# Recurrence and attention in blocks of their own, with gate slabs between their steps

## The chip, the cores and the metric

The kernel runs on one core of a Trainium2 chip (trn2). It is one program in Bass: every engine (PE or TensorE for matmuls, DVE or VectorE, ACT or ScalarE, POOL or GpSimd, SP or SyncE for issuing DMAs) has an instruction list of its own that it works off in order, and the lists are tied together by semaphores. The metric is device time of one execution in microseconds (us); lower is better. The kernel before ran three times: 2592.06, 2585.43 and 2591.16 us, median 2591.16.

## What is computed

One step of a streaming encoder layer for two request groups, a prompt of 1024 tokens and a sample of 64 new tokens after 128 cached ones (1088 tokens together, eight tiles of 128 and one of 64). D_MODEL is 1024. Cut to what matters here:

```python
h = rms_norm(x, pre_mix_gain)
a_q, a_k, a_v, i_q, i_k, i_w, b_q, b_f, b_i, b_g, c_q, gates = split(h @ w_in)   # gates: 3 * 1024 columns
# A: each query keeps its top-k keys by an indexer's score, 6 heads of 128, 2 kv heads
s = where(valid, q @ k_sel * HEAD_DIM ** -0.5, -inf);  y_a = softmax(s) @ v_sel
# B: gated linear recurrence, 6 heads, key and value width 128
f = lower_bound + (1 - lower_bound) * sigmoid(b_f);  b = cumsum(log(f))
o = (q * exp(b)) @ state + (decayed causal scores) @ v
state = exp(b_end) * state + (k * exp(b_end - b)).T @ v
y_b = rms_norm(o, hgrn_norm_gain) * silu(b_g)
# C: cross attention of 4 heads into 256 memory tokens -> y_c
g_a, g_b, g_c = split(sigmoid(gates))
merged = g_a * (y_a @ w_out_a) + g_b * (y_b @ w_out_b) + g_c * (y_c @ w_out_c)
x = x + rms_norm(merged @ w_out, ...);  then a squared-ReLU MLP of width 4096
```

## The kernel before

**Projections.** The program is a row of blocks, and between two blocks all engines meet. `block_project` works through a plan of weight slabs of 256 columns. A slab is loaded (1 MB, SP L172), rounded to its high part `w_hi` by ACT (L179), its low part `w_lo` is made by POOL (L186), and PE makes three products per pair of operands (hi by hi, hi by lo, lo by hi; L199) to keep fp32 accuracy. There are two slab buffers, so a slab's PE work covers the preparation of the next one. A slab of the form "features" has 6 bank units (2 times 128 features, by column groups of 384, 384 and 320 tokens), 24 matmuls each, so 144 matmuls a slab. ACT moves each finished bank to `b_stage` with the slab's function (L513), and SP stores it.

Block b1 makes the indexer's inputs, block b2 (`plan_second`) all the rest: 16 slabs of k, v, q, b_i, c_q, b_g and b_q, then 9 gate slabs with Sigmoid, then 3 slabs of kind "decay", then 3 gate slabs. Beside b2 the indexer runs: PE makes scores, and DVE finds each row's top-k (`index` steps, L753 to L764) and leaves an additive mask in SBUF (`bias`, for all tiles). A decay slab needs DVE for each bank (L564: f from the sigmoid, L567: 1 - f) and for scans of the logarithms (L574), and ACT takes the Ln of its six banks at its end (L519). DVE takes them in its list only behind the last top-k step. The staging buffers `ix_work` and `ix_qT` of the indexer carry the decay results to SP.

**Branches.** `block_branches` then goes over 54 slots, one for each head of each tile (`A_HEADS` = 6). In a slot stand: scores of one attention head (L1013), the mask and maximum on DVE (L1331), Exp on ACT (L1222), the turn of the probabilities on PE (L982), the products with the values once in three heads (L1036), parts of the memory attention, and two steps (one before, one behind the attention's share) of the recurrence. A tile's recurrence has 6 scaling steps (kinds 1, 2, 4, ... 64 with a `k` and a `q` step beside them; `stages(i)`): DVE makes differences `dif` (L1374, L1381, L1384, L1385), ACT takes Exp (L1203 to L1206), POOL multiplies them into `wk` (L1267 to L1276), PE makes 6 small fp32 products (L1090, two records each), and DVE copies the allowed parts into `smat` (L1405). At a tile's end come the output and state products (L1080, L1083, L1097), the mean square (ACT L1233, DVE L1453), its power on POOL (L1293, L1295), the scaling of 6 heads on ACT (L1249), the product with `bg` on POOL (L1300), the turn on PE (L1105) and the store.

**Merge.** `block_merge`'s stage splits y into high and low parts by pieces (ACT L1551, DVE L1589), multiplies by `w_out_a`, `w_out_b`, `w_out_c`, and DVE multiplies each bank by its stored gate (L1598). After it come the output projection and the MLP.

Of the kernel before, what the change touches and what calls it, by code (L numbers as in the profile page):

```python
# [7 lines left out]
P = 128  # L8
D_MODEL, SEQ, DEC, PAST, N_MEM = 1024, 1024, 64, 128, 256
HD, IDX_D = 128, 64  # L10
# [84 lines left out]
def build(nc, io):  # L95
    with ExitStack() as ctx:
# [18 lines left out]

        g.ident = g.sb("ident", [P, P])
        g.gains = g.sb("gains", [P, 3, KT])
        ring_semaphores(g)
        with ExitStack() as mid:
            g.bias = mid.enter_context(nc.sbuf_tensor("bias", [P, BIAS_OFF[N_TILE]], F32))  # L120
            with ExitStack() as first:
                weight_ring(g, first, "w1")
                g.h_hi = first.enter_context(nc.sbuf_tensor("h_hi", [P, KT, T_PAD], F32R))
                g.h_lo = first.enter_context(nc.sbuf_tensor("h_lo", [P, KT, T_PAD], F32R))
                with ExitStack() as c0:
                    g.m_hi = c0.enter_context(nc.sbuf_tensor("m_hi", [P, KT, N_MEM], F32R))
                    g.m_lo = c0.enter_context(nc.sbuf_tensor("m_lo", [P, KT, N_MEM], F32R))
                    plans = plan_first(g), plan_second(g)
                    block_norm(g, plans[0][:2])
                    block_project(g, "b1", plans[0], False, plans[1][:2])  # L130
                block_project(g, "b2", plans[1], True, [])
            block_branches(g)
# [25 lines left out]
def ring_semaphores(g):  # L158
    g.slab = 0
    g.arrived = [g.sem(f"arrived{i}") for i in range(N_TILE + N_MEM // P)]  # L160
    g.w_loaded = [g.sem("w_loaded0"), g.sem("w_loaded1")]
    g.w_rounded = g.sem("w_rounded")
    g.w_split = g.sem("w_split")

# [46 lines left out]
def block_norm(g, ahead):  # L211
    nc, io = g.nc, g.io
    NT = N_TILE + N_MEM // P
    with ExitStack() as ctx:
# [16 lines left out]
        with nc.Block() as block:  # L231
# [49 lines left out]
            def _(dve):  # L281
                nc.vector.memset(ss[:], 1.0).then_inc(zeroed, 1)
                for t in (g.h_hi, g.h_lo):
                    nc.vector.memset(t[:, :, T_ALL:T_PAD].bitcast(F32), 0.0)
# [79 lines left out]
def plan_second(g):  # L364
# [29 lines left out]
    n_late = 3  # L394
    gates = [(g.d_gate[j * 256:], OFF_G + j * 256) for j in range(3 * D_MODEL // 256)]
    for d, off in gates[:-n_late]:
        to_features(d, off, 1, ACT.Sigmoid)
# [4 lines left out]
    for d, off in gates[-n_late:]:  # L402
        to_features(d, off, 1, ACT.Sigmoid)
    return plan


def block_project(g, tag, plan, with_index, ahead):
# [13 lines left out]
    n_out = []  # L421
# [4 lines left out]
    with ExitStack() as ctx:  # L426
# [5 lines left out]
        stored = [g.sem(f"{tag}_stored{j}") for j in range(NS)]  # L432
# [4 lines left out]
        with nc.Block() as block:  # L437
            @block.sync
            def _(sp):
# [26 lines left out]
                for j in range(NS):  # L466
                    sp.wait_ge(stored[j], 16 * per[j])
# [30 lines left out]
            def _(act):  # L498
# [3 lines left out]
                for s, sl in enumerate(plan):  # L502
                    for n in range(first[s], first[s + 1]):
# [6 lines left out]
                        if n >= NS:  # L510
                            act.wait_ge(stored[n % NS], 16 * n_out[n - NS])
# [12 lines left out]
            def _(pe):  # L524
                for s, sl in enumerate(plan):
# [3 lines left out]
                    for n in range(first[s], first[s + 1]):  # L529
# [3 lines left out]
                        if sl.kind == "t":  # L533
                            c = slice(u[0] * P, (u[0] + 1) * P)
                            last = three_products(pe, g.ps[:, n % NB, 0:sl.cols],
# [87 lines left out]
def index_setup(g, ctx):  # L623
# [9 lines left out]
    ix.cnt = sb("ix_cnt", [P, 1])  # L633
    ix.in_, ix.turned, ix.kept, ix.scored = g.sem("ix_in"), g.sem("ix_turned"), g.sem("ix_kept"), g.sem("ix_scored")
# [9 lines left out]
    ix.n_in = 0  # L644
    return ix

# [60 lines left out]
def index_select(g, ix, dve):  # L707
# [32 lines left out]
    for i in range(N_TILE):  # L740
# [23 lines left out]
        link(v.tensor_scalar(sc, left, -1.0, MASKED, ALU.add, ALU.mult))  # L764

# [3 lines left out]
N_HEAD = N_TILE * A_HEADS  # L769
N_SLOT = N_HEAD + 4  # L770
# [9 lines left out]
STEP0 = [sum(len(stages(j)) for j in range(i)) for i in range(N_TILE + 1)]  # L780


def v_tiles(i):

    if i < TILE_P:
        return [(j, P) for j in range(i + 1)]
    return [(TILE_P, P), (TILE_P + 1, DEC)]


def block_branches(g):  # L790
    nc, io = g.nc, g.io
    V, S, G = nc.vector, nc.scalar, nc.gpsimd
    with ExitStack() as ctx:
        sb = lambda name, shape, dt=F32: ctx.enter_context(nc.sbuf_tensor("br_" + name, shape, dt))
# [1280 lines left out]
```

## Time and profile before

The three timed runs gave 2592.06, 2585.43 and 2591.16 us; the profiled execution has a span of 2590.3 us, 0.9 below their median.

| stretch, us | what runs | length, us |
|---|---|---|
| 42 to 183 | block b1 | 141 |
| 183 to 974.3 | block b2, 31 slabs | 791.3 |
| 977.1 to 1445.1 | block_branches | 468.0 |
| 1445.1 to 1691 | merge with the gates | 245.9 |
| 1691 to 2590 | output projection and MLP | 899 |

The profile's list of busy time and its 40 slices of the span (each digit is a busy share in tenths; PEclk the granted clock of TensorE in tenths of full speed):

```profile
PE 2391.7 (92%) x14604; PEld 2208.2 (85%) x14604; DVE 1303.8 (50%) x2275; ACT 724.3 (28%) x1334; POOL 707.6 (27%) x708
...
PE   6999999999999995778888699997999999999998
...
DVE  4113469999960513878777344416332332332335
...
PEclk8999999999999996889999899998999999999999
```

Slices 16 to 22 are the branch block. It is the one long stretch in which PE's digit is below 9.

### The profile page before, as it was taken

What the parts mean: (1) busy time and instruction counts of PE and PEld (TensorE: products, weight loads), DVE (VectorE), ACT (ScalarE), POOL (GpSimd) and SP (SyncE); (2) the same over time, 40 slices, a digit from 0 to 9 for tenths busy, and PEclk for the clock granted to TensorE, in tenths of its full rate; (3) what the DMA queues carried; (4) which work ended last, traced back from release to release, by engine and by line L of the source; (5) the groups of instructions that cost most, each with busy time, mean ns of one, the idle gap of its engine ahead of it and who ended that gap; (6) DMA issues with size and microseconds to landing.
All of it is one profiled execution on the core that took longest, in us unless ns stands there. A gap on an engine that the chain in (4) does not pass through costs nothing. (4 is left out here: it accounts for less than half of the span.)

```text
span 2590.3 us, 36896 instructions
## 1 busy us (share of the span) xinstructions
PE 2391.7 (92%) x14604; PEld 2208.2 (85%) x14604; DVE 1303.8 (50%) x2275; ACT 724.3 (28%) x1334; POOL 707.6 (27%) x708
## 2 busy tenths in 40 slices
PE   6999999999999995778888699997999999999998
PEld 5988799999999994566666599897998998998996
DVE  4113469999960513878777344416332332332335
ACT  5223422222122323444544211224221221221222
POOL 2432332121122113555444222115122122122112
PEclk8999999999999996889999899998999999999999
DMA  4352123222222325322210553314111111111103
GB/s 150 104 146 64 34 78 94 79 93 94 84 95 92 102 98 183 87 61 86 82 45 26 169 182 117 98 68 139 41 49 33 48 49 40 41 49 49 32 33 146
DMA packets 205526, 217.48 MB, mean 84 GB/s; under 512 B 25808, under 2 KB 185616, under 8 KB 205392
## 3 DMA queue, kind: packets, MB, share of 16 engines
q1 hardware_dynamic: 205392, 215.66, 26.4%
q8 instruction: 88, 1.44, 0.2%
q14 instruction: 46, 0.38, 0.0%
HBM read 155.26 MB, written 60.36 MB: 83 GB/s over the span
## 5 line engine op out<-in xcount | busy, mean ns | idle before, releaser
L186 POOL TENSOR_TENSOR w_lo<-w_raw,w_hi 128x2048 fp32r<-128x2048 f32 (+2 forms) x48 | 205.7, 4286 | 824.4 <-ACT w_hi L179 824.4
L199 PE MATMUL ps<-h_hi,w_lo 128*128 128x384 f32 (+1 forms) x960 | 313.1, 326 | 0.0
L199 PE MATMUL ps<-h_lo,w_hi 128*128 128x384 f32 (+1 forms) x960 | 312.9, 326 | 0.0
L199 PE MATMUL ps<-h_hi,w_hi 128*128 128x384 f32 (+1 forms) x960 | 312.8, 326 | 0.0
L1900 POOL TENSOR_TENSOR w_lo<-w_raw,w_hi 128x2048 fp32r<-128x2048 f32 x31 | 142.9, 4609 | 589.3 <-ACT w_hi L1924 589.3
L199 PE MATMUL ps<-w_hi,h_hi 128*128 128x256 f32 x1008 | 288.0, 286 | 7.8 <-PEq L437 4.1
L513 ACT ACTIVATE b_stage<-ps 128x256 f32<-128x256 f32 (+4 forms) x254 | 106.6, 420 | 665.6 <-PE ps L199 665.6
L199 PE MATMUL ps<-w_lo,h_hi 128*128 128x256 f32 x1008 | 287.0, 285 | 0.0
L199 PE MATMUL ps<-w_hi,h_lo 128*128 128x256 f32 x1008 | 286.9, 285 | 0.0
L199 PE MATMUL ps<-f_hi,w_hi 128*128 128x384 f32 (+1 forms) x768 | 251.2, 327 | 2.5 <-POOL ff_u_lo L1896 2.5
L199 PE MATMUL ps<-f_hi,w_lo 128*128 128x384 f32 (+1 forms) x768 | 251.1, 327 | 0.0
L199 PE MATMUL ps<-f_lo,w_hi 128*128 128x384 f32 (+1 forms) x768 | 250.9, 327 | 0.0
L1977 DVE TENSOR_TENSOR big<-big,ps 128x512 f32<-128x512 f32 x144 | 98.9, 687 | 272.0 <-PE ps L199 272.0
L199 PE MATMUL ps<-w_hi,ff_u_lo 128*128 128x512 f32 x576 | 224.2, 389 | 0.0
L199 PE MATMUL ps<-w_lo,ff_u_hi 128*128 128x512 f32 x576 | 224.2, 389 | 0.0
L199 PE MATMUL ps<-w_hi,ff_u_hi 128*128 128x512 f32 x576 | 224.1, 389 | 0.0
L199 PEld LDWEIGHTS ps<-w_hi,h_hi 128*128 128x128 f32 x1008 | 195.5, 194 | 10.9 <-issue 6.7
L1967 DVE TENSOR_TENSOR ff_relu_sq<-ff_relu_sq 128x384 f32<-128x384 f32 (+1 forms) x96 | 83.8, 873 | 238.1 <-ACT ff_relu_sq L1933 237.9
L199 PEld LDWEIGHTS ps<-w_lo,h_hi 128*128 128x128 f32 x1008 | 195.5, 194 | 0.0
L199 PEld LDWEIGHTS ps<-w_hi,h_lo 128*128 128x128 f32 x1008 | 195.3, 194 | 0.0
L199 PEld LDWEIGHTS ps<-h_hi,w_hi 128*128 128x128 f32 x960 | 180.2, 188 | 0.0
L199 PEld LDWEIGHTS ps<-h_hi,w_lo 128*128 128x128 f32 x960 | 180.2, 188 | 0.0
(219 smaller groups left out, 5078.0 us busy)
## 6 DMA issues: line engine op xcount, KB each, us to landing
w_raw<-in_w_in SPq DMA_DIRECT2D x34, 1024.0 KB, 5.6
w_raw<-in_w_up SPq DMA_DIRECT2D x16, 1024.0 KB, 5.5
w_raw<-in_w_down SPq DMA_DIRECT2D x16, 1024.0 KB, 5.1
d_gate<-b_stage SPq DMA_DIRECT2D x48, 192.0 KB, 1.8
gm_gate<-d_gate SPq DMA_DIRECT2D x48, 192.0 KB, 2.6
gm_y_raw<-d_y SPq DMA_DIRECT2D x8, 576.0 KB, 4.5
n_x<-in_x_prompt SPq DMA_DIRECT2D x8, 512.0 KB, 5.8
w_raw<-in_w_mem_kv SPq DMA_DIRECT2D x4, 1024.0 KB, 6.2
```

The lines of the kernel that those rows point to most:

```text
L186: engine.tensor_tensor(g.w_lo[:, s, 0:size], g.w_raw[:, s, 0:size], g.w_hi[:, s, 0:size].bitcast(F32), ALU.subtract).then_inc(g.w_split, 1)
L199: last = pe.matmul(out, left(a, kk), right(b, kk), start=(kk == 0 and n == 0), stop=(kk == k - 1 and n == 2))
L513: nc.scalar.activation(stage[0:r, n % NS, 0:c], g.ps[0:r, n % NB, 0:c], sl.func).then_inc(staged, 1)
L1900: G.tensor_tensor(g.w_lo[:, slot, :], g.w_raw[:, slot, :], g.w_hi[:, slot, :].bitcast(F32), ALU.subtract).then_inc(g.w_split, 1)
L1967: V.tensor_tensor(sq[:, u % 2, 0:n], relu[:, u % 2, 0:n], relu[:, u % 2, 0:n], ALU.mult).then_inc(sq_made, 1)
L1977: V.tensor_tensor(dst, dst, g.ps[:, 4 + d % B_DN, :], ALU.add).then_inc(acc_done, 1)
```

## The change

`block_branches` is taken apart. Three of the twelve gate slabs stay in b2 (2 before the three decay slabs, 1 behind), so that b2 has 22 slabs instead of 31. Four gate slabs are made inside a new `block_recurrence`, five inside a new `block_attention`, by a class `Filler`: it puts a given number of the slabs' matmuls into PE's list between the steps of the block, ACT moves the finished banks out, POOL makes `w_lo` of the next slab (in `block_recurrence` in four pieces of 512 columns), and SP loads and stores. The recurrence block has one step per tick, 80 steps in 86 ticks, with 48 matmuls of the filler first and 6 in each tick. The attention block has the 54 slots, with 96 matmuls first and 12 in each slot; the value products (now one per head) and the memory attention's outputs have PSUM banks of their own.

Further parts: gates are stored without Sigmoid (`ACT.Copy`), and the merge opens them on ACT (`open_gate`); the gain of the recurrence's norm moves from a POOL product (L1289) to a scale in the merge's split, behind a small load `head_gain`; the mask `bias` is stored to DRAM (`store_bias`, 9 DMAs, 2.4 MB) and read back per tile in two buffers; `h_hi` and `h_lo` are cut to 1088 tokens; the level steps' `dif` is one operation of 768, and their Exp two of 384.

```diff
+            gates = plan_gates(g)
+            beside_recurrence, beside_attention = gates[3:7], gates[7:]
+            plans = plan_first(g), plan_second(g, gates[:3])
...
+            block_project(g, "b2", plans[1], True, beside_recurrence[:2])
+            block_recurrence(g, Filler(g, "r", beside_recurrence, beside_attention[:2], [0, 1, 2, 3], 3))
+            block_attention(g, Filler(g, "a", beside_attention, [], [5, 6], 2))
...
-    for d, off in gates[:-n_late]:
-        to_features(d, off, 1, ACT.Sigmoid)
+    for sl in gates[:-1]:
+        plan.append(sl)
...
+                            if n == decays[0]:
+                                store_bias(g, ix, sp)
...
+    def fill(self, pe, count):
+        g, nb = self.g, len(self.banks)
+        for _ in range(count):
+            u, m = divmod(self.mm, self.n_mm)
+            if u == len(self.units):
+                return
+            s, (ft, c0, n, _) = self.units[u]
+            if m == 0:
+                if u % self.per_slab == 0:
+                    pe.wait_ge(g.w_split, self.n0 + s + 1)
+                if u >= nb:
+                    pe.wait_ge(self.evicted, u - nb + 1)
...
+LEAD_IN, PER_TICK = 48, 6
+N_TICK = Q_STEP[-1] + 8
...
+                fl.fill(pe, LEAD_IN)
+                for tick in range(N_TICK):
+                    late = tick in Q_STEP
+                    if late:
+                        fl.fill(pe, PER_TICK)
+                    if tick < len(STEPS):
+                        recur_step(tick)
+                    for i in at(lambda i: STEP0[i + 1], tick):
+                        recur_state(i)
+                    for i in at(lambda i: Q_STEP[i] + 6, tick):
+                        recur_out(i)
+                    if not late:
+                        fl.fill(pe, PER_TICK)
...
+                for n in range(N_SLOT):
+                    i, slot = divmod(n, A_HEADS)
+                    if n < N_HEAD:
+                        scores(n)
+                    fl.fill(pe, PER_SLOT // 2)
...
+                open_gate(0)
+                open_gate(1)
                 for u, (s, b, f, c0, n) in enumerate(units):
+                    if u + 2 < len(units):
+                        open_gate(u + 2)
```

On SP's list in block b2, around the first stores of a decay slab (`d_kk` and `d_cum` are the decay results in DRAM, `d_gate` the gates), the program before has:

```order
L465 DMA d_gate<-b_stage 128x384 x2
L465 DMA d_gate<-b_stage 128x320
L172 DMA w_raw<-in_w_in 128x8x256
L454 DMA d_kk<-ix_work 128x384
L454 DMA d_cum<-ix_qT 128x384
L454 DMA d_kk<-ix_work 128x384
```

After the change the same place, seven slabs earlier in the plan, has the stores of the mask behind the first pair:

```order
L475 DMA d_gate<-b_stage 128x320
L177 DMA w_raw<-in_w_in 128x8x256
L462 DMA d_kk<-ix_work 128x384
L462 DMA d_cum<-ix_qT 128x384
L669 DMA d_bias<-bias 128x128
L669 DMA d_bias<-bias 128x256
...
L669 DMA d_bias<-bias 64x192
```

The mask's stores, the first of which waits for the last top-k step, now stand ahead of the further decay stores and the next slab's load.

On PE's list inside the branch work (`br_wk` is the recurrence's scaled operand, `br_prob` the attention's probabilities), the program before has this, attention and recurrence by turns:

```order
L1013 MATMUL ps<-br_kT,br_qT 128x512
L1048 MATMUL ps<-br_mkT,br_cq 128x256 x2
L1036 MATMUL ps<-br_pT,br_val 128x384 x3
L1090 MATMUL ps<-br_wk 128x128 x6
L982 MATMUL ps<-ident,br_prob 128x128 x4
L1090 MATMUL ps<-br_wk 128x128 x6
```

In the new recurrence block (`hr_wk` is the same operand, L833 the filler's matmul on a gate slab):

```order
L1044 MATMUL ps<-hr_wk 128x128 x6
L833 MATMUL ps<-h_hi,w_hi 128x384
L833 MATMUL ps<-h_lo,w_hi 128x384
L833 MATMUL ps<-h_hi,w_lo 128x384
L833 MATMUL ps<-h_hi,w_hi 128x384
L833 MATMUL ps<-h_lo,w_hi 128x384
L833 MATMUL ps<-h_hi,w_lo 128x384
L1044 MATMUL ps<-hr_wk 128x128 x6
```

What stood between two recurrence steps was attention; now it is six gate matmuls, and the attention follows in a block of its own.

On ACT's list at the start of the merge (`gm_y_hi` is the high part of y, in pieces), the program before has:

```order
L1551 ACTIVATE gm_y_hi<-gm_y_raw 128x2x320 [waits gm_y_in0]
L1551 ACTIVATE gm_y_hi<-gm_y_raw 128x2x320 [waits gm_y_in1]
L1551 ACTIVATE gm_y_hi<-gm_y_raw 128x3x384 [waits gm_y_in0,gm_full]
L179 ACTIVATE w_hi<-w_raw 128x1024 [waits w_loaded0,gm_full]
```

After the change:

```order
L1789 ACTIVATE gm_y_hi<-gm_y_raw 128x2x320 [waits gm_y_in0]
L1789 ACTIVATE gm_y_hi<-gm_y_raw 128x2x320 [waits gm_y_in1]
L1801 ACT_TABLE_LOAD
L1801 ACTIVATE gm_gate<-gm_gate 128x384 [waits gm_gate_in0]
L1801 ACTIVATE gm_gate<-gm_gate 128x384 [waits gm_gate_in1]
```

The sigmoids of the gates, with a table load ahead of the first, stand behind all six pieces of the first split.

## Rows read from the trace of the kernel before

**Rows 1.** Windows of stages: window, length, busy (instructions) of PE, PEld, DVE, ACT, POOL, PEclk, DMA share, GB/s.

```profile
618.60:832.00 213.40, 213.40 (x1297) 213.40 (x1296) 135.93 (x182) 43.10 (x64) 41.63 (x9) 1.00 0.29 92
...
977.10:1002.60 25.50, 11.26 (x44) 7.48 (x44) 2.37 (x7) 9.90 (x20) 0.78 (x2) 0.59 1.01 325
1002.60:1445.10 442.50, 345.10 (x2034) 274.34 (x2034) 340.07 (x758) 197.93 (x457) 227.22 (x178) 0.90 0.23 65
1445.10:1472.00 26.90, 10.77 (x49) 10.13 (x49) 9.19 (x10) 6.95 (x8) 4.72 (x2) 0.67 0.65 202
```

**Rows 2.** Timeline of POOL in block b2, two gate slabs running: start, duration, operation.

```profile
620.92 4.63 POOL L186 TENSOR_TENSOR w_lo<-w_raw,w_hi 128x2048 fp32r<-128x2048 f32 x1 [19.09 <-ACT w_hi L179]
644.65 4.63 POOL L186 TENSOR_TENSOR w_lo<-w_raw,w_hi 128x2048 fp32r<-128x2048 f32 x1 [19.09 <-ACT w_hi L179]
```

**Rows 3.** Timeline of DVE from the last top-k step to the first decay steps.

```profile
758.70 0.25 DVE L764 TENSOR_SCALAR bias<-ix_work 64x192 f32<-64x192 f32 x1
836.87 2.37 DVE L564 TENSOR_SCALAR b_stage<-b_stage,fg_oml,fg_lb 128x384 f32<-128x384 f32 x1 [77.92 <-ACT b_stage L513]
...
840.96 0.48 DVE L564 TENSOR_SCALAR b_stage<-b_stage,fg_oml,fg_lb 128x384 f32<-128x384 f32 x1 [1.32 <-ACT b_stage L513]
```

**Rows 4.** Timeline of ACT at the end of the first decay slab.

```profile
856.26 1.28 ACT L519 ACT_TABLE_LOAD   x1
857.55 2.49 ACT L519 ACTIVATE b_stage<-b_stage 128x384 f32<-128x384 f32 x6
859.95 1.90 ACT L179 ACTIVATE w_hi<-w_raw 128x2048 fp32r<-128x2048 f32 x1
861.87 1.28 ACT L513 ACT_TABLE_LOAD   x1
```

**Rows 5.** Groups of POOL in the branch block: busy, mean ns of one, idle before and its releasers.

```profile
L1276 POOL TENSOR_TENSOR br_wk<-br_bq,br_ex 128x384 f32<-128x384 f32 x48 | 53.7, 1119 | 0.0
L1275 POOL TENSOR_TENSOR br_wk<-br_kk,br_ex 128x384 f32<-128x384 f32 x48 | 51.6, 1076 | 93.4 <-issue 52.1 <-PE ps L1090 31.7 <-ACT br_ex L1206 8.6
L1300 POOL TENSOR_TENSOR br_osb<-br_osb,br_bg 128x768 f32<-128x768 f32 x8 | 16.9, 2107 | 0.0
L1267 POOL TENSOR_TENSOR br_kp<-br_kk,br_exn 128x768 f32<-128x768 f32 x8 | 16.4, 2049 | 74.6 <-ACT br_ex L1204 74.6
L1270 POOL TENSOR_TENSOR br_wk<-br_bq,br_ex 128x768 f32<-128x768 f32 x8 | 14.8, 1855 | 19.2 <-PE ps L1090 19.2
...
L1295 POOL TENSOR_TENSOR br_ms<-br_ms,br_expo 128x6 f32<-128x6 f32 x8 | 11.9, 1488 | 0.7
L1293 POOL TENSOR_SCALAR br_ms<-br_ms 128x6 f32<-128x6 f32 x8 | 4.8, 598 | 0.7
```

**Rows 6.** Groups of DVE in the same stretch.

```profile
L1405 DVE COPY_PREDICATED br_smat<-br_masks,ps 128x384 f32<-128x384 int32 x112 | 62.0, 584 | 35.3 <-PE ps L1090 30.4 <-PE ps L1088 4.1
```

**Rows 7.** Groups of ACT in the same stretch.

```profile
L1206 ACT ACTIVATE br_ex<-br_dif 128x768 f32<-128x768 f32 x56 | 46.2, 840 | 24.8 <-DVE br_dif L1385 19.2 <-POOL br_wk L1268 3.3 <-DVE br_dif L1374 0.8
...
L1249 ACT ACTIVATE br_osb<-br_osb,br_ms 128x128 f32<-128x128 f32 x48 | 14.9, 389 | 41.8 <-POOL br_ms L1295 41.8
```

**Rows 8.** Timeline of PE inside the branch block (an fp32 product is two records).

```profile
1307.83 4.03 PE L1036 MATMUL ps<-br_pT,br_val 128*128 128x384 f32 x12
1311.70 1.50 PE L1090 MATMUL ps<-br_wk 128*128 128x128 f32 x12
...
1315.97 2.63 PE L1090 MATMUL ps<-br_wk 128*128 128x128 f32 x12 [2.00 <-DVE br_smat L1405]
```

**Rows 9.** Windows at the merge's first matmuls, columns as in rows 1.

```profile
1460.00:1463.00 3.00, 3.00 (x11) 3.00 (x10) 0.67 (x1) 0.92 (x2) 0.00 (x0) 0.50 1.06 369
1463.00:1466.00 3.00, 2.32 (x13) 2.00 (x12) 1.40 (x2) 1.83 (x2) 1.94 (x1) 0.99 0.45 139
```

**Rows 10.** Timeline of DVE at the start of the merge.

```profile
1467.17 1.01 DVE L1598 TENSOR_TENSOR big<-ps,gm_gate 128x384 f32<-128x384 f32 x2
```

**Rows 11.** Timeline of ACT there, the last piece of the first split.

```profile
1470.28 0.74 ACT L1551 ACTIVATE gm_y_hi<-gm_y_raw 128x640 fp32r<-128x640 f32 x1 [3.25 <-DMA gm_y_raw<-d_y]
```

More of the change, by code:

```diff
@@ L401, in plan_second, with plan_gates @@
                              [(ft, c0, n, 2 * j + ft) for ft in range(2) for c0, n in GROUPS], ACT.Sigmoid))
[L402 to L404 removed]
+    plan.append(gates[-1])
+    return plan
+def plan_gates(g):
+    w = g.io["w_in"][0]
+    return [SlabPlan("f", w_cols(w, OFF_G + j * 256, 256), 256, feature_units(g.d_gate, j * 256), ACT.Copy)
+            for j in range(3 * D_MODEL // 256)]
 def block_project(g, tag, plan, with_index, ahead):
@@ L431, in block_project @@
         rope_part, rope_done = g.sem(f"{tag}_rope_part"), g.sem(f"{tag}_roped")
-        stored = [g.sem(f"{tag}_stored{j}") for j in range(NS)]
+        stored, before = g.stored, list(g.stored_before)
+        g.stored_before = [b + 16 * k for b, k in zip(before, per)]
         ix = index_setup(g, ctx) if with_index else None
@@ L644, in index_setup, with store_bias @@
     ix.n_in = 0
-    return ix
+    per_tile = [2 if i < 2 else (1 if i < TILE_P else 0) + 2 * ((TOPK_P if i < TILE_P else TOPK_S) // 8) - 1 + 7
+                for i in range(N_TILE)]
+    ix.n_steps = sum(per_tile)
+    return ix
+def store_bias(g, ix, sp):
+    sp.wait_ge(ix.step, ix.n_steps)
+    for i in range(N_TILE):
+        sp.dma_start(g.d_bias[row_slice(i), 0:n_keys(i)],
+                     g.bias[0:rows(i), BIAS_OFF[i]:BIAS_OFF[i + 1]]).then_inc(ix.bias_out, 16)
 def index_loads(g, ix, sp):
@@ L883, in dcount, with at, done_before @@
+        def at(ticks, tick):
+            return [i for i in range(N_TILE) if ticks(i) == tick]
+        def done_before(tick):
+            return min(len(fl.units), (LEAD_IN + PER_TICK * tick) // fl.n_mm)
         def dcount(i, pos):
@@ L1042, in mem_scores @@
-                def mem_scores(i, pair):
-                    r, m = rows(i), 0 if i < TILE_P else 1
-                    pe.wait_ge(s_in[i % 2], N_IN * (i // 2 + 1))
-                    if 2 * i + pair >= 1:
-                        pe.wait_ge(c_exp, 2 * i + pair)
-                    for e in range(2):
-                        last = pe.matmul(g.ps[0:r, 7, e * N_MEM:(e + 1) * N_MEM], cq[:, i % 2, 2 * pair + e, 0:r],
-                                         mkT[:, m, 2 * pair + e, :], start=True, stop=True)
-                    last.then_inc(c_done, 1)
@@ L1549, in split, with open_gate @@
                     raw, hi, _ = piece(m)
+                    b, k0, _, _ = pieces[m]
                     act.wait_ge(y_in[m % 2], 16 * (m // 2 + 1))
-                    nc.scalar.activation(hi, raw, ACT.Copy).then_inc(hi_done, 1)
+                    if b < 2:
+                        nc.scalar.activation(hi, raw, ACT.Copy).then_inc(hi_done, 1)
+                        return
+                    act.wait_ge(head_in, 16)
+                    for k in range(raw.shape[1]):
+                        last = nc.scalar.activation(hi[:, k, :], raw[:, k, :], ACT.Copy,
+                                                    scale=head_gain[:, k0 + k:k0 + k + 1])
+                    last.then_inc(hi_done, 1)
+                def open_gate(u):
+                    n = units[u][4]
+                    act.wait_ge(gate_in[u % NG], 16 * (u // NG + 1))
+                    x = gate[:, u % NG, 0:n]
+                    nc.scalar.activation(x, x, ACT.Sigmoid).then_inc(gate_ok, 1)
                 round_slab(g, act, n0, BRANCHES[0][2] * 256)
```

1061 lines of the change are left out of this document (609 added, 452 removed).

## The prediction

> **What bounds the kernel now.** I read the windows by stage first. In block b2 PE is busy for all of a stretch of gate slabs (213.40 of 213.40 us, first row of [rows 1]), at full clock, so whatever leaves this list shortens it by its own length. In the branch block PE is busy for 345.1 of 442.5 us, DVE for 340.1, and the granted clock is 0.90; ahead of that stand 25.5 us in which PE does 11.3 us of work, at 0.59 ([rows 1]). So over a fifth of that block is not used by PE, and no engine fills it: the steps of the recurrence pass through DVE, ACT, POOL and PE in turn, and each waits for the next. The groups show it: POOL's products at L1275 stood idle for 93.4 us ahead of them, PE's L1090 by DVE's copies [rows 5, 8]. The merge starts with 26.9 us in which PE works 10.8 [rows 1]. The rest (b1, output, MLP) is not touched. The question is therefore whether nine slabs fit into what PE leaves idle. The profiled span is 2590.3 us, 0.9 under the median of 2591.16; the sum is made against 2590.3, and what it says of the median is the same within that.
>
> **Term 1, the second projection.** POOL makes one `w_lo` each 23.73 us (644.65 - 620.92, [rows 2]), which is one slab of 144 matmuls, so 0.165 us a matmul. Nine slabs leave: 9 x 23.7 = 213.4 us.
>
> Against that stands a stall. The nine gate slabs ran from 618.6 to 832.0 (213.4, first row of [rows 1]), and the decay slabs behind them; with two gates instead of nine these begin at 832.0 - 7 x 23.7 = 666.1. DVE takes their banks behind the top-k, which ends at 758.95 [rows 3]; before the change it had been idle for 77.92 us when the first decay bank came [rows 3], so the mask was ready long ahead. Now it is not. PE goes on through the first decay slab (23.7, to 689.8), and into the second until its four free banks are full (4 x 24 x 0.165 = 15.9): it stops at 705.7. The way back: DVE ends at 759.0, takes twelve operations of at most 0.48 (5.4), ACT loads the Ln table and takes six logarithms of 0.42 (the first part of [rows 4]; the last logarithm ends near 764.9 as they follow DVE's banks), rounds the next slab (1.90), loads the Sigmoid table (1.28) and copies the first bank (about 0.5, as a logarithm of the same size takes 0.42): 768.8. PE stands still for 768.8 - 705.7 = 63 us, and restarts at half clock, which I put at 2: at the merge's start the granted clock was 0.50 to 1463 and 0.99 behind it [rows 9]. Below nothing this can't be, since DVE's list fixes the order; above, it could be 70 if the mask's stores (2.4 MB, ahead of the next decay stores on SP) hold the staging buffers. I take no cost for those, as PE has by then 40 us of decay work left to cover them. Net: -213.4 + 63 + 2 = **-148** (-155 to -138).
>
> **Term 2, the branch work.** Before 468.0 us (25.5 + 442.5, [rows 1]). After, two blocks.
>
> Recurrence, per tile of 128. PE: a step is 12 records, and twelve records took 3.87 us at 384 columns (1311.70 - 1307.83, [rows 8]), so 0.108 at 128: 1.3 a step. Seven such steps 9.1, the q step's double 2.6, the k turn, state and output 0.65 + 1.3 + 0.65, and 9 ticks of 6 fills, 54 x 0.165 = 8.9: 23.2. POOL [rows 5]: kind 1 takes 2.05 + 1.85, six levels 6 x (1.12 + 1.08) = 13.2, q 1.86, k about the same (1.82), the power 0.60 + 1.49, the product with `bg` 2.11: 25.0. DVE: 14 mask copies of 0.58 [rows 6], seven differences of 0.96, and some 7 of copies, state and reduction: 22. ACT: 7 x 0.84 x 1.2 and the scalings of 6 x 0.39 [rows 7]: 14.3. POOL is the longest. What it will wait for, by estimate: the mean square behind DVE's state updates 0.9, the next Exp behind the six scalings on ACT 1.0, and kind 1 behind the q step, for which PE has six fills first, 2.7. So 29.8 a tile, an estimate between 25.0 (POOL alone) and 36 (below). Eight tiles 238.4, minus 5 for the first, which has no norm of an older tile. The start is loads 7, a difference 0.96, two Exp 1.7, POOL 3.9, PE 1.5 and 0.4 for semaphores: 15.5, where before POOL's first product came 25.5 us into the block [rows 1]. The sixteen pieces of `w_lo` on POOL are 16 x 1.2 (a quarter of 4.63, [rows 2]) = 19, of which some stand in waits: 14. The tile of 64 and the last tile's chain to its store: 30. Together 15.5 + 238.4 - 5 + 14 + 30 = **293**.
>
> Attention. Its products in 128-column records: scores 450, turns of the probabilities 225, values 450, memory 360, q, k and memory keys 90, less the narrow tile, 1528 x 0.108 = 165. Nothing else is near that: of DVE's 340 busy us [rows 1] the recurrence takes 8 x 22 with it. Fills: 5 x 144 - 96 = 624, x 0.165 = 103; the 96 of the lead-in 15.8; the turns of the keys, which go at ACT's pace, 9.5; waits in the 54 slots 14 (the start's and the last slots' chain Exp, turn, value product). Together **307**.
>
> 293 + 307 - 468 = **+132**. The check: at full clock PE's own work is now 169 + 118 in attention and 121 + 94 in the recurrence, 502 us in 600; before it was 345 + 11 of busy records in 468, many at half clock (12 records in 1.50 us, and again in 2.63, [rows 8]). PE is thus as idle as before (98 us), only in other places; the gain is that the clock holds, since the fills close the gaps.
>
> **Term 3, the merge.** In front of the first product with a gate ACT now has all six splits, then a table load (1.28, [rows 4]) and a Sigmoid of some 0.5. The sixth split began at 1470.28 and took 0.74 [rows 11], the first product began at 1467.17 [rows 10]: 1470.28 + 0.74 + 1.28 + 0.5 = 1472.8, with the semaphores about 1473.4. DVE frees the banks 6 us later, and PE's fifth unit shifts by about 5. `head_gain` ahead of the first load on SP: 1. Behind that, 72 sigmoids of 0.5 = 36 us go into ACT's idle time (it works 7 of 27 us there, [rows 1]). **+6** (+2 to +10). The bias reads in attention (0.5 MB a tile at most, a tile ahead) and the raw stores cost nothing beside PE.
>
> **Sum.** 2590.3 - 148 + 132 + 6 = 2580.3. Forecast **2580**, a gain of 0.4%, with 2565 to 2598 as its own range.
>
> **Rivals.** *R1, the recurrence is held by PE's list.* A step that gets ready just behind the start of six fills waits 6 x 0.165 = 1.0 us, and in the q tick 2.0; if each of the eight ticks pays 0.8, a tile takes 36, the block 50 more: **2630**. It decides slower (by 0.3%) once a tile takes over 29.8 + 18.5 / 8 = 32.1. For it: of POOL's idle time ahead of L1275, 31.7 us were waits for PE [rows 5]. Against: two ticks of a buffer need 2.2 + 1.0 + 1.3 = 4.5 us, less than the two POOL ticks of 3.1 they run beside.
>
> *R2, the clock does not hold.* In the branch block it was 0.90 [rows 1]. If the new blocks grant 0.9 too, PE's work grows by a ninth, and in attention, where PE is the longest, all of that is on the path: 287 x 0.11 = 32, so **2610**. For: the gaps between steps stay, only shorter. Against: where PE had no gap the clock was 1.00 (first row of [rows 1]), and the fills leave it few.
>
> The Trainium skill, TensorE: Matmul & The Clock Gate, section "A second HAM failure mode: psum-queue depth-cycling", tells of a kernel in which short idles between groups of matmuls, as it cycled through its banks, made the clock go up and down. The trace agrees as far as it goes, with 0.90 over a block full of such idles; by this rule the time would be R2's, and by full clock the forecast's.
>
> *R3, the engines overlap better.* POOL waits for nothing but the norm (27 a tile), the pieces of `w_lo` fall in its waits, attention waits only 5: -22 - 9 = **2550**.
>
> *R4, the change does not stall as its lists say.* Were the top-k done 60 us sooner, when PE no longer runs beside it, the stall would shrink to a few us: **2520**. Against: DVE's steps there wait for nothing but each other, so nothing in the wait makes them faster.
>
> **Chances.** Forecast 0.51, R1 0.18, R2 0.10, R3 0.17, R4 0.04. A measurement can tell 0.3% (7.8 us) from no change, so "same" is 2583.4 to 2598.9. Of the forecast's 0.51, 0.27 lie faster, 0.18 the same, 0.06 slower. Faster 0.27 + 0.17 + 0.04 = 0.48, same 0.18, slower 0.34. The range takes in R3 and R1, with the term bounds: 2540 to 2640.
>
> **What would show it.** PE idle by about 63 us from 706 to 769, with DVE in top-k; b2 ends near 826; POOL's kind-1 products 30 us apart from tile to tile; the recurrence 293 and the attention 307 long; PEclk 1.0 in both; the merge's first product with a gate at 28 us into its block. Wrong it goes if PE's steps wait in the fills (R1), or if PEclk is under 0.95 (R2).

## The result and the profile after

The changed kernel takes 2625.94 us (median of 2618.51, 2625.94 and 2628.51), the kernel before 2590.93: a ratio of 1.013, with an interval of 1.0108 to 1.0152. A fourth run of the changed kernel took 2995.68 us at a granted clock of 0.741 instead of 0.95 to 0.96 (the slow state) and is left out. The forecast was 2580, a little faster; the kernel became 1.3% slower. The time lies inside the stated range of 2540 to 2640, near the rival R1 in size, but not by R1's mechanism, as the runs below show.

The profiled execution of the changed kernel has a span of 2626.5 us, 36.2 more than before. Its page, the lines that answer to those shown of before:

```profile
PE 2393.6 (91%) x14908; PEld 2230.8 (85%) x14908; DVE 1295.9 (49%) x2232; ACT 768.6 (29%) x1471; POOL 710.7 (27%) x723
...
PE   6999999999738888879999699998999999999998
...
DVE  3113479999994777604444345515422332332335
...
PEclk8999999999869999979999799998999999999999
```

The busy sums of PE, DVE and POOL hardly moved (ACT has 44 us more), and the span grew. In PE's row a 7 and a 3 stand in slices 11 and 12, where b2 had nines, and 8s in the recurrence; only attention's middle is full.

SP issues the first load of each new block at its start, so three rows of its timeline (start, duration, operation) cut the span into its parts: the recurrence's first load, attention's, the merge's.

```profile
826.40 0.37 SPq L968 DMA_DIRECT2D hr_cum<-d_cum  x1
...
1141.78 0.38 SPq L1354 DMA_DIRECT2D at_room<-out_new_k_prompt  x1
...
1473.94 0.37 SPq L1755 DMA_DIRECT2D gm_head_gain<-in_hgrn_norm_gain  x1
```

| part | before | after | change | forecast |
|---|---|---|---|---|
| up to the branch work | 977.1 | 826.4 | -150.7 | -148 |
| recurrence | | 315.4 | | 293 |
| attention | | 332.2 | | 307 |
| branch work together | 468.0 | 647.5 | +179.5 | +132 |
| merge to the end | 1145.2 | 1152.6 | +7.4 | +6 |
| sum | 2590.3 | 2626.5 | +36.2 | -10 |

Two of the three terms hold within 3 us. The whole miss is in term 2: 22 us in the recurrence and 25 in attention (22 in five other kernels, in which the same attention block took 328.7 to 329.2).

Windows of the changed kernel, columns as in [rows 1]: the decays' stall, the decays, most of the recurrence, then attention's start, its middle and its end, and the merge's start.

```profile
705.70:769.00 63.30, 2.76 (x9) 2.77 (x10) 61.22 (x96) 7.32 (x11) 4.53 (x1) 0.52 0.08 30
769.00:823.80 54.80, 54.47 (x329) 54.21 (x327) 30.22 (x70) 19.28 (x32) 9.38 (x2) 0.99 0.62 208
...
842.00:1000.00 158.00, 129.57 (x893) 122.68 (x891) 115.94 (x166) 61.98 (x125) 139.15 (x100) 0.92 0.35 103
...
1141.80:1165.00 23.20, 18.49 (x100) 18.24 (x100) 0.00 (x0) 3.40 (x5) 5.00 (x4) 0.87 0.91 297
...
1300.00:1440.00 140.00, 136.27 (x882) 118.52 (x881) 60.49 (x174) 61.45 (x136) 5.30 (x4) 1.00 0.17 52
1440.00:1473.90 33.90, 29.39 (x166) 23.13 (x164) 9.37 (x37) 10.24 (x38) 0.00 (x0) 0.79 0.10 27
1473.90:1503.00 29.10, 13.35 (x56) 12.71 (x57) 10.00 (x10) 10.08 (x13) 4.70 (x2) 0.72 0.54 161
```

The stall stands where it was forecast: 2.8 us of PE work between 705.7 and 769, while DVE works for 61.2. The last top-k step and ACT's way back, in the timelines of DVE and ACT (the answer to [rows 3, 4]):

```profile
757.13 0.25 DVE L789 TENSOR_SCALAR bias<-ix_work 64x192 f32<-64x192 f32 x1
757.42 0.48 DVE L576 TENSOR_SCALAR b_stage<-b_stage,fg_oml,fg_lb 128x384 f32<-128x384 f32 x1
```

```profile
762.49 1.89 ACT L184 ACTIVATE w_hi<-w_raw 128x2048 fp32r<-128x2048 f32 x1
764.40 1.28 ACT L525 ACT_TABLE_LOAD   x1
765.69 1.20 ACT L525 ACTIVATE b_stage<-ps 128x384 f32<-128x384 f32 x3
```

DVE takes the first decay bank 0.04 us behind the last mask step, and the first copy that frees PE stands at 765.7 (forecast 768.3).

POOL's groups and DVE's in the recurrence (842 to 1115 us, the answer to [rows 5]). A tile of 128 has nine steps: kind 1, six levels (2 to 64), `q` and `k`; the "6 scaling steps" of the section on the kernel before are the levels alone.

```profile
L1154 POOL TENSOR_TENSOR hr_wk<-hr_kk,hr_ex 128x384 f32<-128x384 f32 x47 | 56.1, 1195 | 8.2 <-issue 6.2 <-PE ps L1042 1.9
...
L864 POOL TENSOR_TENSOR w_lo<-w_raw,w_hi 128x512 fp32r<-128x512 f32 x16 | 24.3, 1521 | 0.0
L1151 POOL TENSOR_TENSOR hr_wk<-hr_kk,hr_ex 128x768 f32<-128x768 f32 x8 | 19.0, 2381 | 5.5 <-ACT hr_ex L1101 5.5
...
L1147 POOL TENSOR_TENSOR hr_wk<-hr_bq,hr_ex 128x768 f32<-128x768 f32 x7 | 17.0, 2430 | 0.0
```

```profile
L1212 DVE TENSOR_TENSOR hr_dif<-hr_cum 128x768 f32<-128x768 f32 x53 | 72.8, 1374 | 0.5 <-ACT hr_ex L1105 0.5
...
L1206 DVE TENSOR_TENSOR hr_dif<-hr_cum 128x768 f32<-128x768 f32 x8 | 15.6, 1954 | 0.0
```

POOL has little idle time left in front of its level products (8.2 us, where [rows 5] had 93.4), but a product of 768 now takes up to 2.43 us on average instead of the 1.86 to 2.11 of [rows 5], and a piece of `w_lo` 1.52 where 1.2 was taken. The first and the second tile's first products, and the last tile's, give the tile:

```profile
835.48 2.50 POOL L1146 TENSOR_TENSOR hr_kp<-hr_kk,hr_exn 128x768 f32<-128x768 f32 x1 [8.30 <-ACT hr_ex L1099]
...
866.16 2.52 POOL L1146 TENSOR_TENSOR hr_kp<-hr_kk,hr_exn 128x768 f32<-128x768 f32 x1
...
1093.59 1.01 POOL L1146 TENSOR_TENSOR hr_kp<-hr_kk,hr_exn 128x384 f32<-128x384 f32 x1 [1.24 <-PE ps L1037]
```

(1093.59 - 835.48) / 8 = 32.3 us a tile, pieces included, and from the last row to the end of the block 48 us.

### The profile page after: what moved, and what is told of

Its sections match the earlier page's. It is cut to its first block and busy times, and to the rows that moved or that the text cites. A ratio compares the mean times of both kernels' runs of the same rounds, so it can differ in the third digit from the quotient of the medians.

```text
span 2626.5 us, 37816 instructions
## 1 busy us (share of the span) xinstructions
PE 2393.6 (91%) x14908; PEld 2230.8 (85%) x14908; DVE 1295.9 (49%) x2232; ACT 768.6 (29%) x1471; POOL 710.7 (27%) x723
## 5 line engine op out<-in xcount | busy, mean ns | idle before, releaser
L191 POOL TENSOR_TENSOR w_lo<-w_raw,w_hi 128x2048 fp32r<-128x2048 f32 (+2 forms) x40 | 166.8, 4169 | 908.1 <-ACT w_hi L184 908.1
L204 PE MATMUL ps<-w_hi,h_hi 128*128 128x256 f32 (+1 forms) x1008 | 287.4, 285 | 8.2 <-PEq L445 4.5
L204 PE MATMUL ps<-w_lo,h_hi 128*128 128x256 f32 (+1 forms) x1008 | 286.4, 284 | 0.0
L204 PE MATMUL ps<-w_hi,h_lo 128*128 128x256 f32 (+1 forms) x1008 | 286.3, 284 | 0.0
L204 PE MATMUL ps<-h_hi,w_hi 128*128 128x384 f32 (+1 forms) x528 | 173.0, 328 | 62.5 <-ACT b_stage L525 62.5
L204 PEld LDWEIGHTS ps<-w_hi,h_hi 128*128 128x128 f32 (+1 forms) x1008 | 189.1, 188 | 11.0 <-issue 6.8
L204 PEld LDWEIGHTS ps<-w_lo,h_hi 128*128 128x128 f32 (+1 forms) x1008 | 189.1, 188 | 0.0
L204 PEld LDWEIGHTS ps<-w_hi,h_lo 128*128 128x128 f32 (+1 forms) x1008 | 188.9, 187 | 0.0
L833 PE MATMUL ps<-h_hi,w_hi 128*128 128x384 f32 (+1 forms) x432 | 167.2, 387 | 8.6 <-PEq L960 5.6
L204 PE MATMUL ps<-h_hi,w_lo 128*128 128x384 f32 (+1 forms) x528 | 173.0, 328 | 0.0
L204 PE MATMUL ps<-h_lo,w_hi 128*128 128x384 f32 (+1 forms) x528 | 172.9, 327 | 0.0
L778 DVE MAX8 ix_m<-ix_work 128x8 f32<-128x384 f32 (+6 forms) x191 | 168.2, 881 | 6.6
```

What stands on the lines that cost most here:

```text
L191: engine.tensor_tensor(g.w_lo[:, s, 0:size], g.w_raw[:, s, 0:size], g.w_hi[:, s, 0:size].bitcast(F32), ALU.subtract).then_inc(g.w_split, 1)
L204: last = pe.matmul(out, left(a, kk), right(b, kk), start=(kk == 0 and n == 0), stop=(kk == k - 1 and n == 2))
L778: link(v.max(m8, sc if it == 0 else left))
L833: last = pe.matmul(g.ps[:, self.banks[u % nb], 0:n], w[:, m // 3, ft * P:(ft + 1) * P], x[:, m // 3, c0:c0 + n], start=(m == 0), stop=(m = ...
```

## The experiments

Three questions were put: what a filled slab costs in each block, what bounds a recurrence tile, and what the stall in b2 is worth. The times of blocks below are from SP's rows as above, in one profiled execution of each kernel. They have a spread of their own: where a run leaves a block as it is in the changed kernel, the recurrence took 312.9 to 315.4 us (four kernels), attention 328.7 to 332.2 (six) and everything from the merge on 1147.8 to 1154.7 (ten). Smaller differences of a block say nothing.

### No filler in the recurrence

```diff
-            beside_recurrence, beside_attention = gates[3:7], gates[7:]
+            beside_recurrence, beside_attention = gates[3:3], gates[7:12]
```

> The changed kernel with no filler in the recurrence block: four gate slabs are left out (the merge reads three stored slabs in their place). The block took 315 us with them. Theory POOL: POOL's list is the longest of the block (busy for about 235 of the 258 us between the first and the last tile's first product), and a slab in the filler costs its four pieces of w_lo there (24 us for 16 pieces) and a piece of the end: the block takes about 277, the kernel 2589. Rival PE list: the steps wait behind the fills, so that without them a tile takes 26 instead of 32.3: 250, the kernel 2560. Rival clock: without fills PE falls to 1.2 GHz in the gaps, a step takes 2.6 instead of 1.3, and the block is no shorter than 315.

Measured: 2615.2 us, the recurrence 304.2 (1132.71 - 828.49), a tile 31.4. None of the three came out. SP's rows at its two ends:

```profile
828.49 0.37 SPq L968 DMA_DIRECT2D hr_cum<-d_cum  x1
...
1132.71 0.38 SPq L1354 DMA_DIRECT2D at_room<-out_new_k_prompt  x1
```

Its window in the middle of the block, beside that of the changed kernel (the second fence):

```profile
860.00:1090.00 230.00, 149.37 (x942) 140.24 (x942) 175.34 (x253) 82.67 (x172) 187.87 (x136) 0.83 0.25 68
```

```profile
860.00:1090.00 230.00, 188.90 (x1300) 178.95 (x1300) 170.86 (x249) 92.33 (x188) 201.58 (x144) 0.93 0.33 95
```

POOL is idle for 42 us of 230 and PE for 81, so without fills neither is the bound; the steps pass through all engines at a lower clock (0.83 against 0.93). Four slabs in the filler cost the block 315.4 - 304.2 = 11.2 us, 2.8 each. In the recurrence the filler is nearly free. What costs is the block itself.

### The filler's matmuls alone

```diff
+                def idle_fill(count):
+                    for _ in range(count):
+                        m = dummy[0] % 24
+                        w_hi = slab_view(g, fl.n0, KT, 256)[0]
+                        pe.matmul(g.ps[:, dummy[0] // 24 % 4, 0:384], w_hi[:, m // 3, 0:P], g.h_hi[:, m // 3, 0:384],
+                                  start=True, stop=True)
+                        dummy[0] += 1
...
-                        fl.fill(pe, PER_TICK)
+                        idle_fill(PER_TICK)
```

> The recurrence block with the filler's matmuls alone: PE multiplies a weight slab that lies there, with the same count and place (48 first, 6 a tick), nothing is moved out, split, loaded or stored for it (four gate slabs are left out, the merge reads stored ones). With the real filler the block took 315.4 us, with none 304.2 at a granted clock of 0.83. Theory pieces: the matmuls hold the clock and cost POOL nothing, so POOL's list without its 24 us of pieces sets the tile at 29 and the block takes 285 to 292. Rival PE list: the matmuls themselves hold the steps, and the block takes 305 or more.

Measured: the recurrence 297.2 (1122.89 - 825.74), a tile 30.9, the clock 0.95:

```profile
860.00:1090.00 230.00, 197.14 (x1383) 186.71 (x1382) 180.11 (x265) 84.48 (x177) 193.24 (x142) 0.95 0.25 69
```

It is 5 us over the range of the pieces theory and 8 under that of the rival, which is R1's. The matmuls do not hold the steps: with them the block is 7 us shorter than without. Nothing else was added, and the granted clock is 0.95 in place of 0.83, so the gain is read as the clock's; it is what R1 had wrong. The real filler's other parts (pieces on POOL, evictions on ACT, the end) cost 315.4 - 297.2 = 18.2.

### DVE's differences taken away

```diff
-                    V.tensor_tensor(d3, b3, ref.to_broadcast([P, nb, 2 * kind]), ALU.subtract).then_inc(d_done, 1)
+                    V.tensor_tensor(d3[:, 0:1, 0:1], b3[:, 0:1, 0:1], ref[:, 0:1, :], ALU.subtract).then_inc(d_done, 1)
```

> The changed kernel with DVE's differences in the recurrence cut to one element each (the rest of the array is zero, so the recurrence's values are not computed); all waits stay. DVE gets some 10 us a tile less work. Theory shared access: POOL's products of 768 run in 1.82 us again instead of 2.0 to 2.4, the Exp of the k step no longer waits for a difference of 2, and the block takes 315 - 8 x (1.3 + 1.5) = 293. Rival: the durations stay, since they come from POOL itself, and the block moves by no more than the k step's wait, to 308.

Measured: the recurrence 284.7 (1111.13 - 826.40), 30.7 less, and a tile 28.6. The theory had the way right and the size too small, by 8 us. POOL's product of the k step in its groups, against 2381 ns in the changed kernel:

```profile
L1153 POOL TENSOR_TENSOR hr_wk<-hr_kk,hr_ex 128x768 f32<-128x768 f32 x8 | 14.7, 1835 | 5.1 <-ACT hr_ex L1103 5.1
```

POOL's durations fell to what they are undisturbed, so DVE's differences had lengthened them. Two pairs in the timeline of the kernel without filler show it from both sides:

```profile
961.92 1.80 POOL L1146 TENSOR_TENSOR hr_kp<-hr_kk,hr_exn 128x768 f32<-128x768 f32 x1 [0.67 <-PE ps L1037]
...
962.26 2.28 DVE L1212 TENSOR_TENSOR hr_dif<-hr_cum 128x768 f32<-128x768 f32 x1
...
972.40 0.95 DVE L1212 TENSOR_TENSOR hr_dif<-hr_cum 128x768 f32<-128x768 f32 x1
```

A difference that POOL leaves alone takes 0.95 us; one that begins during a POOL product of 1.80 takes 2.28: it ends 0.82 us behind the product's end (964.54 against 963.72), a little under its own length. The pairs are no exceptions. Of the 64 differences of 768 in the changed kernel's recurrence, the ten that began with POOL idle took 0.94 to 0.96 us, and 37 that began in a POOL product or piece ended 0.81 or 0.82 behind its end. Seven that began in the power's product of 6 elements (L1167) were not lengthened: 0.93 to 0.96. The run also shortened DVE's list and the Exp's wait for it (DVE was busy for 141.7 of 230 us instead of 170.9), and the granted clock was 0.98 instead of 0.93, so the 31 us are all of these together, and how they divide is open.

### The differences in two operations

```diff
-                    V.tensor_tensor(d3, b3, ref.to_broadcast([P, nb, 2 * kind]), ALU.subtract).then_inc(d_done, 1)
+                    V.tensor_tensor(d3[:, :, 0:kind], b3[:, :, 0:kind], ref.to_broadcast([P, nb, kind]), ALU.subtract)
+                    V.tensor_tensor(d3[:, :, kind:], b3[:, :, kind:], ref.to_broadcast([P, nb, kind]),
+                                    ALU.subtract).then_inc(d_done, 1)
```

> The changed kernel with the differences of the level steps as two DVE operations of 384, as the kernel before has them, instead of one of 768. If DVE and POOL hinder each other by the time that DVE's differences run (mean 1.37 us for 768 where an undisturbed one takes 0.94), two operations of together 1.5 us hinder POOL as much or more: the recurrence 5 to 15 longer, the kernel 2632 to 2642. Rival: DVE is not on the path of POOL, 2627.

Measured: 2626.5 us, ratio to before 1.0138 (1.0121 to 1.0155), the recurrence 316.6 (1144.58 - 827.94). DVE gets more work (202.5 of 230 us busy instead of 170.9), and nothing moves beyond the spread: the rival's number. Its reason, that DVE is not on the path of POOL, does not hold beside the run before. What it costs POOL does not follow from DVE's busy time alone; POOL's own even fell (193.8 instead of 201.6). The one form or the other is not what made the kernel slower.

### A product moved from POOL to DVE

```diff
-                        pool.wait_ge(o_normed, i + 1)
-                        pool.wait_ge(v_in[i % 2], 32 * (i // 2 + 1))
-                        G.tensor_tensor(o, o, bg[0:rows(i), i % 2, :], ALU.mult).then_inc(y_done, 1)
...
+                        dve.wait_ge(o_normed, i + 1)
+                        dve.wait_ge(v_in[i % 2], 32 * (i // 2 + 1))
+                        V.tensor_tensor(o, o, bg[0:rows(i), i % 2, :], ALU.mult).then_inc(y_done, 1)
```

> The product of the normed output with bg (2.18 us a tile on POOL) moved to DVE in the recurrence block. Theory POOL: POOL sets the tile, so eight tiles give 8 x 2.2 = 17 us: the kernel 2610. Rival PE list or chain: the tile does not move, 2627 (or longer, as DVE gets 1 us a tile more).

Measured: 2612.71 us, ratio 1.0091 (1.0063 to 1.012); the recurrence 303.0, 12.4 shorter for 17 us taken from POOL, which is the theory within 3 us. With the filler in place POOL's list is the longest, as the prediction had it.

### One slab beside attention instead of five

```diff
-            beside_recurrence, beside_attention = gates[3:7], gates[7:]
+            beside_recurrence, beside_attention = gates[3:7], gates[7:8]
...
-LEAD_IN_A, PER_SLOT = 96, 12
+LEAD_IN_A, PER_SLOT = 96, 2
```

> The changed kernel with one gate slab in the attention block in place of five (four left out, the merge reads stored ones). The block took 332 us. Theory PE: attention is a list of PE work without gaps, so four slabs of 23.7 and their switches leave it: about 235, the kernel 2530. Rival chain: once the fills are gone, the chain scores, mask, Exp, turn, value product sets the slot and the clock falls: 270 or more, the kernel 2565.

Measured: 2546.4 us, attention 251.8 (1392.66 - 1140.88). Four slabs cost 80.4, 20.1 each (19.3 by the 329 us of the other kernels), of the 23.7 that one cost in b2. So attention hides about 4 us of a slab. The block lies between the two theories (235, and 270 or more).

### More of the filler ahead of attention

```diff
-LEAD_IN_A, PER_SLOT = 96, 12
+LEAD_IN_A, PER_SLOT = 180, 10
```

> The changed kernel with 180 matmuls of the filler ahead of attention and 10 a slot, in place of 96 and 12 (the same 720). Theory ends: attention is PE work of 283 us at full clock and loses 49, of which 16 stand at its start (a gap of 4.7 for the keys' load and half clock behind it) and 18 at its end (no fills in the last four slots). With more fills ahead and some in the last slots both shrink: 332 becomes 316 to 322, the kernel 2613. Rival: the chain in the slots sets the pace, so that 14 us more of fills at the start are on the path: 332 to 340, the kernel 2630.

Measured: 2625.11 us, ratio 1.013 (1.011 to 1.015); attention 330.5 instead of 332.2. A miss: 316 to 322 was expected, and 1.7 us less is within the spread. In PE's waits of this kernel the gap for the keys' turns had gone, and a new one stood in its place, behind ACT's eviction of the filler's banks.

```profile
PE ps L833 <- ACT af_stage L850: 5.0, 1, 5.0
```

The ends of attention are not mended by moving fills. That a part of the 25 us stands at attention's ends is located by the trace, not shown by a run that removes it.

### The stall filled

```diff
-            beside_recurrence, beside_attention = gates[3:7], gates[7:]
-            plans = plan_first(g), plan_second(g, gates[:3])
+            beside_recurrence, beside_attention = gates[6:10], gates[10:12]
+            plans = plan_first(g), plan_second(g, gates[:6])
...
-LEAD_IN_A, PER_SLOT = 96, 12
+LEAD_IN_A, PER_SLOT = 96, 4
```

> Three gate slabs moved from the attention block to b2 ahead of the decay slabs (six in b2, four beside the recurrence, two beside attention, with 4 fills a slot in place of 12). Nothing is left out. Theory stall: PE idles 63 us in b2 for the top-k, and three slabs are 71 us of work, so b2 ends 8 us later (834), and attention loses 71 and some switches: 332 becomes 257, the kernel 2627 + 8 - 75 = 2560. Rival: attention gives back only 30 as its waits grow with fewer fills: 2605.

Measured: 2567.47 us, ratio 0.9912 (0.9889 to 0.9936), faster than before. Where PE had worked 2.8 of 63 us it now has no gap:

```profile
705.00:769.00 64.00, 64.00 (x393) 64.00 (x392) 61.95 (x99) 19.36 (x28) 14.09 (x3) 1.00 0.28 96
```

b2 ends 5 us later with 71 us of work more, the recurrence is the same (315.3), attention 267.0. It came 7 us above the theory and far from the rival. A slab is thus nearly free ahead of the decays, up to the stall's length, as it is in the recurrence by the run without filler.

### Six slabs in the recurrence, none in attention

```diff
+            beside_recurrence, beside_attention = gates[6:12], gates[12:12]
...
-LEAD_IN, PER_TICK = 48, 6
+LEAD_IN, PER_TICK = 48, 9
```

> Six gate slabs in b2 (five ahead of the decays), six in the recurrence block (9 fills a tick), none in attention; nothing left out. Theory: a slab costs b2 23.7 less the stall it fills, the recurrence some 3 to 6, attention 20. So b2 to 831, recurrence 321 to 328, attention 332 - 5 x 20 = 232 (or 240 if the chain sets it), the rest 1152: the kernel 2545. Rival PE list: 9 fills a tick hold the steps by 1.5 us instead of 1.0, the tile goes to 36, the block to 350: 2570.

Measured: 2553.9 us, ratio 0.9853 (0.9837 to 0.9869), between the theory (9 above it) and the rival (16 below it). The recurrence 329.9, attention 235.4:

```profile
832.55 0.37 SPq L968 DMA_DIRECT2D hr_cum<-d_cum  x1
...
1162.45 0.38 SPq L1354 DMA_DIRECT2D at_room<-out_new_k_prompt  x1
...
1397.83 0.37 SPq L1755 DMA_DIRECT2D gm_head_gain<-in_hgrn_norm_gain  x1
```

Two slabs more cost the recurrence 14.6, 7.3 each, two and a half times the first four's price, and still a third of attention's.

### The same with two small moves

```diff
+                        dve.wait_ge(o_normed, i + 1)
+                        dve.wait_ge(v_in[i % 2], 32 * (i // 2 + 1))
+                        V.tensor_tensor(o, o, bg[0:rows(i), i % 2, :], ALU.mult).then_inc(y_done, 1)
...
                     if m == 2:
                         round_slab(g, act, n0 + 1, BRANCHES[0][2] * 256)
-                open_gate(0)
-                open_gate(1)
+                        open_gate(0)
+                        open_gate(1)
```

> As r6_a0, with the product by bg on DVE and the first two sigmoids of the merge behind the third piece of the split instead of the sixth. Theory: the first gives 12 us as it did with four slabs, the second 3 to 5: 15 below r6_a0, so 2530. Rival: with 9 fills a tick PE has taken POOL's place as the longest, and the move to DVE gives nothing: 4 below r6_a0.

Measured: 2541.85 us, ratio 0.9819 (0.9797 to 0.9841), 12 below the run before, where the theory had 15 and the rival 4: 7.2 in the recurrence (322.7) and 6.6 from the merge on. The latter is no more than that stretch's spread: 1148.1 us, and a kernel without the move had 1147.8. What the move did for certain is the first product with a gate, which stands 19.5 us into the block instead of 23.5 to 25.5. With the next kernel, which is equal to it, this is the fastest of the study, with nothing left out, 1.8% below the kernel before.

### The pieces on DVE as well

```diff
-                        fl.split_piece(pool)
+                        fl.split_piece(dve)
```

> Six gate slabs in b2, six in the recurrence, none in attention, the product by bg on DVE, the first sigmoids earlier (2541.85 on its chip), and the 24 pieces of w_lo in the recurrence block on DVE instead of POOL. Theory POOL: 24 x 1.4 = 34 us leave POOL's list of a block of 323, half of which stood in waits as in the runs before: 15 less, 2527. Rival: DVE, busy 179 of 230 us there, has no room, or PE at 9 fills a tick is the longest: 2540 or more.

Measured: 2541.25 us, ratio 0.981 (0.9792 to 0.9828): the rival. POOL waited 14.0 us for the k step's Exp, which waits for DVE's difference (5.5 in the kernel before it), and the recurrence took 321.3 instead of 322.7.

```profile
POOL hr_wk L1151 <- ACT hr_ex L1101: 14.0, 7, 2.4
```

## Why the prediction was wrong, step by step

The step that failed is term 2's sum: 293 for the recurrence, measured 315.4, and 307 for attention, measured 332.2.

**Term 1 held.** -148 was forecast, -150.7 measured. That the decays would overtake the top-k, the stall of 63 us, its place and the restart at half clock all came as worked out. DVE ended its top-k 1.5 us earlier than before (757.4 against 758.95), and the mask's stores cost nothing, as said: from 769 to the last matmuls of b2 PE was busy for 54.47 of 54.80 us.

**Term 3 came out in number, its mechanism in part.** +6 forecast, +7.4 measured, and by the ten kernels with the same merge +2.6 to +9.5. The first product with a gate stands 25.3 us into the block (28 forecast, 22.1 before), so the wait that the term is made of grew by 3.2 and not by 6; where the rest arises is open, and that the sum fits is in part luck. The product waits for the gate, which stands behind the table and the sigmoids, in the timelines of DVE and ACT:

```profile
1499.22 1.02 DVE L1862 TENSOR_TENSOR big<-ps,gm_gate 128x384 f32<-128x384 f32 x2 [5.79 <-ACT gm_gate L1801]
```

```profile
1497.30 1.28 ACT L1801 ACT_TABLE_LOAD   x1
1498.60 1.97 ACT L1801 ACTIVATE gm_gate<-gm_gate 128x384 f32<-128x384 f32 x4
```

That the sigmoids held this product is shown by `best1`: with two of them earlier it stood at 19.5, without a wait for ACT.

**Term 2 failed, by its sizes in the recurrence (three of them) and in attention.**

*POOL's durations* (25.0 a tile; with the waits of 4.6 that makes 29.6, and the prediction wrote 29.8). They were read in a block in which DVE's differences were spread among attention's work. In the new one the differences follow each other as POOL's products do, and each waits for the other's operation in flight (`dif_tiny`). With the filler's matmuls alone POOL was busy 193.2 of 230 us, 26.0 a tile of 30.9. With the waits (4.9 a tile, forecast 4.6) the tile without pieces was 30.9 and not 29.8. The sum of the waits was right, but not the list: the largest in that run was the k step's Exp (14.6 us in 230), which the prediction did not have. That is luck.

*The pieces* (14 of 19 us). They took 24.3 us at 1.52 each. All of the filler but its matmuls, the pieces among it, cost 18: 11 in the eight tiles, 7 at the end. Together with the durations the eight tiles took 258.1 us instead of 247.4.

*The end.* From the last tile's first product to the block's end 48 us were measured, where the sum had some 36 (30, and what the start's 15.5 has behind its first product): 41 of them with the matmuls alone, and 7 more for the filler's last bank, its 24 matmuls, most of them at half clock (one each 0.27 us), its eviction and its store. 11 in the tiles and 12 at the end are the 22 us.

*Attention.* 283 us of PE work at full clock (165 + 103 + 15.8) took 332. Counted by stretches at the prediction's own prices (0.165 a fill, 0.108 a record of 128 columns), the first 38 us held 112 fills and 48 records, 24 us of work; the middle 260 us held 568 and 1371, 241 us; the last 34 held 40 and 109, 18 us. The prediction had allowed 24 of these 49 us, with the ends at full clock; PE's clock was 0.87 at its start and 0.79 at its end (the windows above), and the two ends lost 30 us together. The middle lost the other 19 at a clock of 1.00; no run tested why.

*The check that should have warned.* It set PE's 502 us of work against 600 and called PE as idle as before. It compared the new blocks with PE's work, not with the block before. (Two slips beside it decide nothing: ACT's terms in the recurrence make 9.4 a tile and not 14.3, and R2's 32 us on 2580 are 2612.) The runs give the accounts: the recurrence without any filler takes 304.2 and attention without any 235.4, together 539.6, where the two by turns took 468.0. **Taking them apart costs 72 us** before a single slab is put in. The prediction's own terms without the filler's, 293 - 14 and 307 - 103 - 15.8, make 467, as if it cost nothing; its price for the nine slabs, 133 us, was 25 above the measured 108. 72 less 25 is the miss of 47. That each had been the other's filler is the reading of this. It fits the granted clock, 0.78 and 0.91 in the two blocks against 0.88 by turns, but a second start and a second end are in the 72 as well (in the bare recurrence 9 us to POOL's first product, and 44 from the last tile's first product to the end), and no run divides them. Four slabs in the recurrence add 11, five in attention 97; 72 + 11 + 97 is the +180 of the table. The gain of 213 us in b2 had to pay for these 180 and for the stall of 63.

**The rivals.** R1 named one of the two blocks and the wrong engine: the filler's matmuls make the recurrence shorter, by 7 us, at a granted clock of 0.95 instead of 0.83. That the time lies near R1's 2630 is chance. R2 was half right: the granted clock was 0.92 in the recurrence and 1.00 in attention's middle, so the bulk of attention lost nothing to it. The rule beside it, from the Trainium skill, TensorE: Matmul & The Clock Gate, section "A second HAM failure mode: psum-queue depth-cycling", agrees in kind with the recurrence's 0.83 without fills and 0.95 with them. Attention's middle is no test of it: PE was busy there for 136.27 of 140 us, and the clock was full. R3 did not come (the tile took 30.9 without the pieces, and not 27), R4 neither (PE stood still for 62.5 us).

## What to carry to other kernels

Before a filler is put beside a chain, ask what fills it now: here two chains stood by turns in one block, and taking them apart cost 72 us, a third of what the move brought. A unit of filler has a price in each place (2.8 us in the recurrence for the first four and 7.3 for two more, about 20 in attention, 1.7 in the stall that the change itself had opened, against 23.7 alone), and the same twelve slabs dealt out by these prices turned a loss of 1.3% into a gain of 1.5%, with two small moves 1.8%. A duration read from a block in which the neighbours are spread does not hold in one in which they run side by side.

## What was not expected of the hardware

DVE's fp32 differences of 128x768, with both operands in SBUF, and POOL's fp32 products and pieces of the same kind hardly ran side by side. The difference took 0.95 us alone and 2.28 when it began 0.34 us into a POOL product of 1.80; in the changed kernel 37 of 64 ended 0.81 or 0.82 behind the POOL operation in which they began. The other way round, POOL's products of 768 in the recurrence took 1.79 to 1.85 us with no such difference in flight at their start (one 2.13), and 2.49 to 2.61 with one. The k step's product fell from 2.38 to 1.83 us on average when the differences were reduced to one element, and the block by 30.7 us of 315.4, in which the shorter list of DVE and the higher clock have a share.

Matmuls that nobody needs, put between the recurrence's steps, made the block shorter: 297.2 us with them and 304.2 without, at a granted clock of 0.95 and 0.83.
